# Encoder trunk on one core: x is turned before it is normalised, its loads are cut in halves, and the start of each layer is put in another order

## The chip, the cores and the metric

The kernel runs on one core of one Trainium2 chip. A core has TensorE (PE: matmuls and transposes, with PEld for its weight loads), VectorE (DVE), ScalarE (ACT), GpSimd (POOL) and SyncE (SP, which here only issues transfers). The metric is device time in microseconds (us), the median of several executions. One further execution was profiled; its span and rows are what the prediction works with.

## The reference

Input x is 256 tokens by 1024 features, f32. There are two layers; then a last RMS norm.

```python
for l in range(DEPTH):
    h = rms_norm(x, norm1_g[l])            # x * rsqrt(mean(x*x) + eps) * gain
    (aq, ..., k_rope) = jnp.split(h @ w_in[l], cuts, axis=-1)      # 1024 x 2144
    # four attentions o_a .. o_d from these, each 256 wide
    y = jnp.einsum('bsnc,ncd->bsnd', br, w_branch[l])
    g = jax.nn.sigmoid(h @ w_gate[l] + b_gate[l])                  # 1024 x 4096
    x = x + jnp.sum(g * y, axis=2) @ w_o[l]
    h2 = rms_norm(x, norm2_g[l])
    x = x + jnp.square(jax.nn.relu(h2 @ w_ff1[l])) @ w_ff2[l]
return rms_norm(x, final_g)
```

The root 1/sqrt(mean + eps) is one number for each token, so it can be multiplied in before a product with a weight matrix or behind it; the gain is one number for each feature.

## The kernel before

**Products.** All weights are f32 and are streamed once for each layer. Each is taken as a high part (`w_hi`, rounded to the matmul's f32r format) and the rest (`w_lo`), and so is each activation (`act_hi`, `act_lo`). A product is three matmuls: high by high, high by low, low by high (`split_product`, L1249 to L1251).

**Weight chunks.** A layer's weights come in chunks of about 1.05 MB, each as two halves. SP loads a half into `raw` (two chunks of room) as soon as DVE has split what stood there; ACT writes `w_hi` (`split_hi`, L603), and DVE writes `w_lo = raw - w_hi` (`split_lo`, L853). The first eight chunks are `w_in`, 268 columns each (`"in"`); a half of such a chunk holds four of the eight row blocks `kc`. Then come the gate and branch chunks, `w_o`, and the MLP.

**Start of a layer.** x lies as `xs` (128 tokens by 1024, twice: t = 0 and 1). ACT takes the sum of squares (`square_sum`, L613), POOL makes the root `rstd` (`norm`, L514 and L515), DVE and ACT scale x into `h` (L860 and L619), PE turns `h` by 128 x 128 transposes against an identity that is loaded first (`turn`, L1260) into four PSUM banks, ACT makes `act_hi` with the gain (`turned_hi`, L627 or L635), DVE makes `act_lo` (`turned_lo`, L871 or L880). Then PE forms chunk 0 by tokens 0 and 1 (`project`), chunk 1, and so on. The gains lie in `vec_all`: rows that were loaded, turned by PE (L1605) and copied (L1112). In the first layer `act_hi` and `act_lo` are made for both token blocks at once, 256 columns each. `keep_warm` issues matmuls whose result nobody reads. The sums of chunk j are taken out of PSUM by ACT for t = 0 (`in_evac`, L640) and by DVE for t = 1 (L1141).

**End of a layer.** The MLP's last two chunks are summed in eight parts of six matmuls with 512 columns (`mlp_out_last`). DVE adds each finished quarter to `xs` (`residual`, L892). In the first layer's end PE turns `h` of token block 0 in the middle of the last part, and block 1 inside the next layer's chunk 1 (`project_next_layer`).

**Order.** Each engine has its own program, written out by hand in this file, and works strictly in that order; a counter (semaphore) is waited for where one needs another's result. There is no scheduler. The gate stage adds the bias in `gate_add` (L1062); POOL loads the first two bias rows (`gate_bias`, L520) behind the root.

## Time and profile before

| | us |
|---|---|
| median of 3 runs | 827.41 (827.32 to 827.42) |
| profiled execution, device time | 827.35 |
| its span, first to last instruction | 825.5 |
| PE busy in the span | 813.9 |
| DVE, ACT, POOL busy | 549.8, 415.6, 56.6 |
| read from memory | 143.49 MB, 175 GB/s over the span |

The device time is 1.85 us above the span. Times in the rows count from the span's start. In a timeline row the first number is the start, the second how long it took (several of one kind merged, with their count at x), then engine, line, operation, output<-inputs, shape; in brackets how long the engine had been idle and whom it waited for.

### The profile page before, as it was taken

What the parts mean: (1) busy time and instruction counts of PE and PEld (TensorE: products, weight loads), DVE (VectorE), ACT (ScalarE), POOL (GpSimd) and SP (SyncE); (2) the same over time, 40 slices, a digit from 0 to 9 for tenths busy, and PEclk for the clock granted to TensorE, in tenths of its full rate; (3) what the DMA queues carried; (4) which work ended last, traced back from release to release, by engine and by line L of the source; (5) the groups of instructions that cost most, each with busy time, mean ns of one, the idle gap of its engine ahead of it and who ended that gap; (6) DMA issues with size and microseconds to landing.
All of it is one profiled execution on the core that took longest, in us unless ns stands there. A gap on an engine that the chain in (4) does not pass through costs nothing.

```text
span 825.5 us, 12984 instructions
## 1 busy us (share of the span) xinstructions
PE 813.9 (99%) x4835; PEld 701.8 (85%) x4835; DVE 549.8 (67%) x803; ACT 415.6 (50%) x698; POOL 56.6 (7%) x97
## 2 busy tenths in 40 slices
PE   7999999999999999999999999999999999999996
PEld 7997777877899999999899877678878999999995
DVE  6667768867676665555767577688774776555663
ACT  6455765664454444333563576658544544333442
POOL 2430000000010000000023200000000100000000
PEclk9999999999999999999999999999999999999999
DMA  8976653554357555565556747346344575566531
GB/s 275 230 232 201 182 179 108 153 170 157 103 173 234 172 173 175 193 203 203 173 149 194 250 163 216 105 139 172 106 168 129 187 243 171 188 203 202 180 126 52
DMA packets 85659, 145.14 MB, mean 176 GB/s; under 512 B 5036, under 2 KB 54448, under 8 KB 85616
## 3 DMA queue, kind: packets, MB, share of 16 engines
q1 hardware_dynamic: 82912, 137.12, 51.5%
q0 software_dynamic: 2496, 7.36, 3.3%
q8 instruction: 27, 0.44, 0.2%
q14 instruction: 16, 0.13, 0.1%
q10 hardware_dynamic: 208, 0.08, 0.0%
HBM read 143.49 MB, written 1.05 MB: 175 GB/s over the span
## 4 chain that ended last, share of the span: by engine, by line
PE 96%; DVE 1%; ACT 1%; POOL 1%; DMA 0%; issue 0%; POOLq 0%; ACTq 0%
PE bank_w L1249 20%; PE bank_w L1251 20%; PE bank_w L1250 20%; PE bank_acc L1249 8%; PE bank_acc L1250 8%; PE bank_acc L1251 8%; PE bank_acc L1345 2%; PE bank_o L1375 2%; PE bank_acc L1358 2%; DVE w_lo L853 1%; DMA cst<-in_table 0%; PE bank_acc L1260 0%; PE bank_x L1306 0%; PE bank_x L1327 0%; PE bank_x L1322 0%; POOL rstd L515 0%
## 5 line engine op out<-in xcount | busy, mean ns | idle before, releaser
L853 DVE TENSOR_TENSOR w_lo<-raw,w_hi 128x1024 fp32r<-128x1024 f32 (+1 forms) x256 | 301.9, 1228 | 61.8 <-ACT w_hi L603 61.4
L603 ACT ACTIVATE w_hi<-raw 128x1024 fp32r<-128x1024 f32 (+1 forms) x256 | 256.4, 1057 | 35.1 <-DMA raw<-in_w_gate 11.0
L1249 PE MATMUL bank_w<-w_hi,act_hi 128*128 128x268 f32 (+1 forms) x512 | 178.1, 348 | 0.1
L1251 PE MATMUL bank_w<-w_hi,act_lo 128*128 128x268 f32 (+1 forms) x512 | 173.9, 340 | 0.0
L1250 PE MATMUL bank_w<-w_lo,act_hi 128*128 128x268 f32 (+1 forms) x512 | 173.6, 339 | 0.0
L1251 PE MATMUL bank_w<-act_hi,w_lo 128*128 128x256 f32 x496 | 141.3, 285 | 0.0
L1250 PE MATMUL bank_w<-act_lo,w_hi 128*128 128x256 f32 x496 | 140.8, 284 | 0.0
L1249 PE MATMUL bank_w<-act_hi,w_hi 128*128 128x256 f32 x496 | 139.8, 282 | 0.0
L743 ACT ACTIVATE part_hi<-big 128x512 fp32r<-128x512 f32 x32 | 20.2, 633 | 189.2 <-DVE big L1095 186.5
L1249 PEld LDWEIGHTS bank_w<-w_hi,act_hi 128*128 128x128 f32 x512 | 96.2, 188 | 15.8 <-issue 6.2
L1251 PEld LDWEIGHTS bank_w<-w_hi,act_lo 128*128 128x128 f32 x512 | 96.2, 188 | 11.1
L1250 PEld LDWEIGHTS bank_w<-w_lo,act_hi 128*128 128x128 f32 x512 | 96.3, 188 | 10.2 <-issue 0.5
L1249 PE MATMUL bank_acc<-w_hi,part_hi 128*128 128x512 f32 x256 | 100.3, 392 | 0.0
L1250 PE MATMUL bank_acc<-w_lo,part_hi 128*128 128x512 f32 x256 | 100.3, 392 | 0.0
L1251 PE MATMUL bank_acc<-w_hi,part_lo 128*128 128x512 f32 x256 | 99.8, 390 | 0.0
L1095 DVE SCALAR_TENSOR_TENSOR big<-bank_w,root_row 128x512 f32<-128x512 f32 x30 | 20.7, 691 | 113.3 <-PE bank_w L1251 113.3
L1249 PEld LDWEIGHTS bank_w<-act_hi,w_hi 128*128 128x128 f32 x496 | 94.2, 190 | 1.2
L1250 PEld LDWEIGHTS bank_w<-act_lo,w_hi 128*128 128x128 f32 x496 | 93.5, 188 | 1.3
L1251 PEld LDWEIGHTS bank_w<-act_hi,w_lo 128*128 128x128 f32 x496 | 93.8, 189 | 0.0
L1251 PEld LDWEIGHTS bank_acc<-w_hi,part_lo 128*128 128x128 f32 x256 | 48.1, 188 | 10.6
L1249 PEld LDWEIGHTS bank_acc<-w_hi,part_hi 128*128 128x128 f32 x256 | 48.1, 188 | 9.5
L1250 PEld LDWEIGHTS bank_acc<-w_lo,part_hi 128*128 128x128 f32 x256 | 48.0, 188 | 8.9
(193 smaller groups left out, 890.5 us busy)
## 6 DMA issues: line engine op xcount, KB each, us to landing
raw<-in_w_ff SPq DMA_DIRECT2D x128, 512.0 KB, 4.9
raw<-in_w_gate SPq DMA_DIRECT2D x64, 512.0 KB, 4.7
raw<-in_w_in SPq DMA_DIRECT2D x32, 536.0 KB, 5.4
raw<-in_w_o SPq DMA_DIRECT2D x16, 512.0 KB, 4.5
gate_row<-in_b_gate POOLq DMA_DIRECT2D x16, 256.0 KB, 4.4
raw<-in_w_branch SPq DMA_DIRECT2D x16, 256.0 KB, 4.4
raw<-in_w_branch SPq DMA_DIRECT2D x8, 512.0 KB, 4.5
xs<-in_x SPq DMA_DIRECT2D x2, 512.0 KB, 4.2
```

Source lines behind the costliest of these rows:

```text
L603: nc.scalar.activation(half_view(w_hi, c, h), raw_half(c, h), ACT.Copy).then_inc(w_hi_ready, 1)
L743: nc.scalar.activation(part_hi[:, b, :, :].rearrange("p k s -> p (k s)"), relu[b], ACT.Square).then_inc(u_hi_ready, 1)
L853: nc.vector.tensor_tensor(half_view(w_lo, c, hf), raw_half(c, hf), f32(half_view(w_hi, c, hf)), ALU.subtract).then_inc(w_lo_ready, 1)
L1095: ins = nc.vector.scalar_tensor_tensor(out=relu[b].rearrange("p (d s) -> p d s", d=2), in0=bank_w[:, b, :].rearrange("p (d s) -> p d s", d ...
L1249: nc.tensor.matmul(dst, s_hi, m_hi, start=first, stop=False)
L1250: nc.tensor.matmul(dst, s_hi, m_lo, start=False, stop=False)
L1251: ins = nc.tensor.matmul(dst, s_lo, m_hi, start=False, stop=last)
L1345: ins = nc.tensor.matmul(bank_acc[:, half, keys], q[:, t * P:(t + 1) * P], k, start=True, stop=True)
L1358: ins = nc.tensor.transpose(bank_acc[:, 2 + b, at:at + P], prob[:, b, t, kt * P:(kt + 1) * P], ident)
L1375: ins = nc.tensor.matmul(bank_o[half * HD:(half + 1) * HD, blk * SEQ:(blk + 1) * SEQ], v, probT[:, half, kt, :], start=(kt == 0), stop=(kt ...
```

## The change

1. **x is turned raw.** `xs` itself is turned; `h`, its scaling on DVE and ACT (L860, L619) and the wait of PE for the root are gone at the start of both layers. The root is multiplied in later: where ACT and DVE take the sums of `w_in` out of PSUM, and in `gate_add`.
2. **Loads of the first layer.** x comes in four pieces of 128 x 512: both left halves, then the first half of chunk 0, then SP waits for the first piece, then both right halves, then the second half of chunk 0. The gain rows of the first norm are waited for alone; the others are turned later, behind chunk 1.
3. **First layer's order.** The five matmuls of `keep_warm` at the start are gone (two stay ahead of chunk 0). PE turns the left halves, takes the left half of chunk 0 by token block 0 in the order four high by high, four by `w_lo`, four by `act_lo`, turns the right halves, takes the left half for block 1, and so on. ACT and DVE make six `act_hi` / `act_lo` ahead of the second half of chunk 0, two behind it. Two of the four squares stand behind that.
4. **Second layer's order.** PE turns the quarters of x behind the residuals, between the parts of the MLP's last sum and between the first products; DVE's two splits of chunk 1 stand between the residuals, and its `act_lo` between them too.
5. POOL loads the first two gate bias rows behind the last small weight of the stage (`w_ukv`).

```diff
-PIECE_OF_FIRST = [(0, 0, D), (1, 0, D)]
+PIECES_OF_FIRST = [(0, 0, 512), (1, 0, 512), (0, 512, D), (1, 512, D)]
+FIRST_TURNED = [3, 4, 7, 8]
 SP:
+            load_x(0)
+            load_half(0, 0, 0)
+            sp.wait_ge(x_landed[0][0], 16)
+            load_x(1)
+            load_half(0, 1, 0)
 POOL:
                 norm(2 * l, l)
-                pool.wait_ge(gate_read, l * GATE_N)
-                for g in range(2):
-                    gate_bias(l, g)
 ...
                 pool.dma_start(w_ukv[:, :], d_w_ukv[bass.ds(l, 1)].rearrange("o k n -> (o k) n")).then_inc(lat_landed, 16)
+                pool.wait_ge(gate_read, l * GATE_N)
+                for g in range(2):
+                    gate_bias(l, g)
 ACT, in_evac:
+                if j == 0:
+                    act.wait_ge(rstd_ready, 2 * l * T + 1)
                 nc.scalar.activation(qkv[:, 0, j * IN_C:(j + 1) * IN_C], bank_w[:, in_bank(j, 0, l), 0:IN_C],
-                                     ACT.Copy).then_inc(in_act, 1)
+                                     ACT.Copy, scale=rstd[:, 0:1]).then_inc(in_act, 1)
 ACT, first layer:
             split_hi_half(0, 0, 0)
             act.wait_ge(vec_ready, 1)
-            turned_hi_both(0, G1, 0, range(0, KD // 2))
+            turned_hi_first(range(0, 6))
             split_hi_half(0, 1, 0)
-            turned_hi_both(0, G1, 0, range(KD // 2, KD))
-            split_hi(1, 0)
+            turned_hi_first(range(6, KD))
+            square_sum(0, 2)
+            split_hi_half(1, 0, 0)
+            square_sum(0, 3)
             in_evac(0, 0)
+            split_hi_half(1, 1, 0)
             split_hi(2, 0)
 ACT, second layer:
+                    turned_hi(2 * l, G1, l, 0, range(0, KD // 2))
                     square_sum(2 * l, 0)
+                    turned_hi(2 * l, G1, l, 0, range(KD // 2, KD))
                     square_sum(2 * l, 1)
-                    scale_right(2 * l, 0)
-                    turned_hi(2 * l, G1, l, 0, range(KD))
+                    in_evac(0, l)
 ...
 DVE, gate_add:
-                nc.vector.tensor_tensor(gate_slot(g // 2, 2 * t + g % 2), bank_w[:, t, :], gate_row[:, g % 2, :],
-                                        ALU.add).then_inc(gate_read, 1)
+                nc.vector.scalar_tensor_tensor(out=gate_slot(g // 2, 2 * t + g % 2), in0=bank_w[:, t, :],
+                                               scalar=rstd[:, t:t + 1], in1=gate_row[:, g % 2, :], op0=ALU.mult,
+                                               op1=ALU.add).then_inc(gate_read, 1)
 DVE, first layer:
-            for t in range(T):
-                scaled(0, t, 0).then_inc(h_ready, 1)
-                scaled(0, t, 1).then_inc(h_right_ready, 1)
+            gains(1, 0, DEPTH * KD)
             dve.wait_ge(vec_ready, 1)
             split_lo_half(0, 0, 0)
-            turned_lo_both(0, G1, 0, range(0, KD // 2))
+            turned_lo_first(range(0, 6))
             split_lo_half(0, 1, 0)
-            turned_lo_both(0, G1, 0, range(KD // 2, KD))
-            split_lo(1, 0)
+            turned_lo_first(range(6, KD))
+            split_lo_half(1, 0, 0)
+            split_lo_half(1, 1, 0)
 PE, new:
+            def turn_first(t, m):
+                pe.wait_ge(x_landed[t][m], 16)
+                turn(xs, t, 0, range(m * KD // 2, (m + 1) * KD // 2))
+            def project_high_parts_first(kcs):
+                pe.wait_ge(w_hi_ready, kcs[0] // (KD // 2) + 1)
+                for kc in kcs:
+                    pe.wait_ge(h_hi_ready, 2 * (kc + 1))
+                    nc.tensor.matmul(dst, act_hi[:, kc, tok], hi[:, kc, :], start=kc == 0, stop=False)
+                pe.wait_ge(w_lo_ready, kcs[0] // (KD // 2) + 1 + 2 * RAW)
+                for kc in kcs:
+                    nc.tensor.matmul(dst, act_hi[:, kc, tok], lo[:, kc, :], start=False, stop=False)
+                for kc in kcs:
+                    pe.wait_ge(h_lo_ready, 2 * (kc + 1))
+                    ins = nc.tensor.matmul(dst, act_lo[:, kc, tok], hi[:, kc, :], start=False, stop=kc == KD - 1)
             def project_first_layer():
-                for hf, kcs in enumerate((left, right)):
-                    pe.wait_ge(w_lo_ready, hf + 1 + 2 * RAW)
-                    project(0, 0, 0, kcs, [2 * (kc + 1) for kc in kcs])
-                    project(0, 1, 0, kcs)
+                project_high_parts_first(left)
+                turn_first(0, 1)
+                turn_first(1, 1)
+                project(0, 1, 0, left)
+                project_high_parts_first(right)
+                project(0, 1, 0, right)
 PE, mlp_out_last:
                 part(a, 2)
+                if l + 1 < DEPTH:
+                    turn_x(2 * l + 2, 0)
                 part(a, 3).then_inc(w_used, 1)
+                if l + 1 < DEPTH:
+                    turn_x(2 * l + 2, 1)
                 part(b, 2).then_inc(acc_done, 1)
-                if l + 1 < DEPTH:
-                    part(b, 3, (0,))
-                    turn_h(l + 1, 0)
-                    part(b, 3, (1,)).then_inc(w_used, 1)
 PE, start:
-            keep_warm(5)
-            turn_h(0, 0)
 ...
+            turn_first(0, 0)
+            turn_first(1, 0)
+            pe.wait_ge(rows_landed, 16)
+            turn_rows(DEPTH * KD)
             keep_warm(2)
```

**DVE at the first layer's start, before.** `xs`, `big` (holds `h`) and `rstd` as above.

```order
L860 TENSOR_SCALAR big<-xs,rstd 128x512 [waits rstd_ready] x4
L1112 COPY vec_all<-bank_acc 128x38 [waits rows_turned]
L853 TENSOR_TENSOR w_lo<-raw,w_hi 128x1072 [waits w_hi_ready,vec_ready]
L880 SCALAR_TENSOR_TENSOR act_lo<-bank_o,vec_all,act_hi 128x256 [waits h_hi_ready] x2
L880 SCALAR_TENSOR_TENSOR act_lo<-bank_x,vec_all,act_hi 128x256 [waits h_hi_ready] x2
L853 TENSOR_TENSOR w_lo<-raw,w_hi 128x1072 [waits w_hi_ready]
L880 SCALAR_TENSOR_TENSOR act_lo<-bank_acc,vec_all,act_hi 128x256 [waits h_hi_ready] x4
L853 TENSOR_TENSOR w_lo<-raw,w_hi 128x1072 [waits w_hi_ready] x2
L1141 COPY qkv<-bank_w 128x268 [waits w_used]
```

The same place with the change (line numbers are those of the changed file).

```order
L1114 COPY vec_all<-bank_acc 128x16 [waits rows_turned]
L865 TENSOR_TENSOR w_lo<-raw,w_hi 128x1072 [waits w_hi_ready,vec_ready]
L882 SCALAR_TENSOR_TENSOR act_lo<-bank_o,vec_all,act_hi 128x256 [waits h_hi_ready] x2
L882 SCALAR_TENSOR_TENSOR act_lo<-bank_x,vec_all,act_hi 128x256 [waits h_hi_ready] x2
L882 SCALAR_TENSOR_TENSOR act_lo<-bank_acc,vec_all,act_hi 128x256 [waits h_hi_ready] x2
L865 TENSOR_TENSOR w_lo<-raw,w_hi 128x1072 [waits w_hi_ready]
L882 SCALAR_TENSOR_TENSOR act_lo<-bank_acc,vec_all,act_hi 128x256 [waits h_hi_ready] x2
L865 TENSOR_TENSOR w_lo<-raw,w_hi 128x1072 [waits w_hi_ready] x2
L1148 TENSOR_SCALAR qkv<-bank_w,rstd 128x268 [waits rstd_ready,w_used]
```

The four scalings ahead are gone, and the second half's split of chunk 0 now stands behind six `act_lo` instead of four.

**PE at the first layer's start, with the change.** Before, the first product (L1249) stood behind all sixteen transposes and waited for `h_lo_ready` and `w_lo_ready`.

```order
L1267 MATMUL bank_o<-cst,xs 128x128 [waits x_landed1_0]
L1267 MATMUL bank_o<-cst,xs 128x128
L1267 MATMUL bank_x<-cst,xs 128x128 x2
L1627 MATMUL bank_acc<-cst,vec_rows 128x16 [waits rows_landed]
L1248 MATMUL bank_w<-cst 128x128 x2
L1401 MATMUL bank_w<-w_hi,act_hi 128x268 [waits h_hi_ready,w_hi_ready]
L1401 MATMUL bank_w<-w_hi,act_hi 128x268 [waits h_hi_ready] x3
L1404 MATMUL bank_w<-w_lo,act_hi 128x268 [waits w_lo_ready]
L1404 MATMUL bank_w<-w_lo,act_hi 128x268 x3
L1407 MATMUL bank_w<-w_hi,act_lo 128x268 [waits h_lo_ready] x4
L1267 MATMUL bank_acc<-cst,xs 128x128 [waits x_landed0_1]
```

The transposes of the right halves, and with them `act_hi` 4 to 7, now stand behind the four products with `act_lo` of the left half.

**DVE between the layers, before.**

```order
L853 TENSOR_TENSOR w_lo<-raw,w_hi 128x1072 [waits w_hi_ready] x4
L892 TENSOR_TENSOR xs<-xs,bank_acc 128x512 [waits acc_done] x2
L860 TENSOR_SCALAR big<-xs,rstd 128x512 [waits rstd_ready]
L892 TENSOR_TENSOR xs<-xs,bank_acc 128x512 [waits acc_done]
L871 SCALAR_TENSOR_TENSOR act_lo<-bank_o,vec_all,act_hi 128x128 [waits h_hi_ready] x2
L871 SCALAR_TENSOR_TENSOR act_lo<-bank_x,vec_all,act_hi 128x128 [waits h_hi_ready] x2
L892 TENSOR_TENSOR xs<-xs,bank_acc 128x512 [waits w_used]
```

With the change.

```order
L865 TENSOR_TENSOR w_lo<-raw,w_hi 128x1072 [waits w_hi_ready] x2
L894 TENSOR_TENSOR xs<-xs,bank_acc 128x512 [waits acc_done]
L865 TENSOR_TENSOR w_lo<-raw,w_hi 128x1072 [waits w_hi_ready]
L894 TENSOR_TENSOR xs<-xs,bank_acc 128x512 [waits acc_done]
L865 TENSOR_TENSOR w_lo<-raw,w_hi 128x1072 [waits w_hi_ready]
L873 SCALAR_TENSOR_TENSOR act_lo<-bank_o,vec_all,act_hi 128x128 [waits h_hi_ready] x2
L873 SCALAR_TENSOR_TENSOR act_lo<-bank_x,vec_all,act_hi 128x128 [waits h_hi_ready] x2
L894 TENSOR_TENSOR xs<-xs,bank_acc 128x512 [waits acc_done]
```

The first residual no longer stands behind four splits but behind two, and nothing here waits for the root.

## Rows read from the trace of the kernel before

**Rows 1.** The page: busy time of PE, and the chain by engine.

```profile
PE 813.9 (99%) x4835; PEld 701.8 (85%) x4835; DVE 549.8 (67%) x803; ACT 415.6 (50%) x698; POOL 56.6 (7%) x97
...
PE 96%; DVE 1%; ACT 1%; POOL 1%; DMA 0%; issue 0%; POOLq 0%; ACTq 0%
```

**Rows 2.** All waits of PE in the span: us in total, times, longest.

```profile
PE bank_w L1241 <- DMA cst<-in_table: 4.7, 1, 4.7
PE bank_o L1260 <- DVE big L860: 0.4, 1, 0.4
```

**Rows 3.** Timeline of PE, the first 12 us.

```profile
4.71 2.50 PE L1241 MATMUL bank_w<-cst 128*128 128x128 f32 x10 [4.71 <-DMA cst<-in_table]
...
7.63 0.64 PE L1260 MATMUL bank_x<-cst,big 128*128 128x128 f32 x2
8.05 1.06 PE L1260 MATMUL bank_acc<-cst,big 128*128 128x128 f32 x4
9.04 0.33 PE L1605 MATMUL bank_acc<-cst,vec_rows 38*128 38x38 f32 x1
...
11.03 0.61 PE L1241 MATMUL bank_w<-cst 128*128 128x128 f32 x4
11.69 0.36 PE L1249 MATMUL bank_w<-w_hi,act_hi 128*128 128x268 f32 x1
```

**Rows 4.** Timeline of ACT, the first 12 us.

```profile
7.76 1.10 ACT L603 ACTIVATE w_hi<-raw 128x1072 fp32r<-128x1072 f32 x1 [0.78 <-DMA raw<-in_w_in]
10.11 0.84 ACT L635 ACTIVATE act_hi<-bank_o,vec_all 128x256 fp32r<-128x256 f32 x2 [1.25 <-PE bank_o L1260]
```

**Rows 5.** Timeline of DVE, the first 24 us.

```profile
9.41 0.20 DVE L1112 COPY vec_all<-bank_acc 128x38 f32<-128x38 f32 x1 [0.33 <-PE bank_acc L1605]
9.64 1.27 DVE L853 TENSOR_TENSOR w_lo<-raw,w_hi 128x1072 fp32r<-128x1072 f32 x1
11.06 0.87 DVE L880 SCALAR_TENSOR_TENSOR act_lo<-bank_o,vec_all,act_hi 128x256 fp32r<-128x256 f32 x2 [0.15 <-ACT act_hi L635]
...
17.92 0.44 DVE L1141 COPY qkv<-bank_w 128x268 f32<-128x268 f32 x1
...
23.85 0.44 DVE L1141 COPY qkv<-bank_w 128x268 f32<-128x268 f32 x1 [3.13 <-PE bank_w L1251]
```

**Rows 6.** A stretch: length, busy time by engine, granted clock, DMA share, GB/s.

```profile
6.50:7.00 0.50, 0.50 (x4) 0.42 (x2) 0.40 (x1) 0.48 (x2) 0.07 (x1) 1.00 1.13 374
```

**Rows 7.** Timeline of DVE between the layers.

```profile
405.68 4.83 DVE L853 TENSOR_TENSOR w_lo<-raw,w_hi 128x1072 fp32r<-128x1072 f32 x4 [0.23 <-ACT w_hi L603]
410.42 1.27 DVE L892 TENSOR_TENSOR xs<-xs,bank_acc 128x512 f32<-128x512 f32 x2
413.47 0.48 DVE L860 TENSOR_SCALAR big<-xs,rstd 128x512 f32<-128x512 f32 x1 [1.77 <-POOL rstd L515]
...
416.79 1.12 DVE L871 SCALAR_TENSOR_TENSOR act_lo<-bank_acc,vec_all,act_hi 128x128 fp32r<-128x128 f32 x4
```

**Rows 8.** Timeline of ACT and of POOL between the layers.

```profile
411.13 0.63 ACT L613 ACTIVATE qkv<-xs 128x512 f32<-128x512 f32 x1 [2.53 <-DVE xs L892]
...
412.89 0.55 POOL L515 TENSOR_TENSOR rstd<-mean,neg_half 128x1 f32<-128x1 f32 x1
```

**Rows 9.** Timeline of PE between the layers.

```profile
413.24 0.40 PE L1251 MATMUL bank_acc<-w_hi,part_lo 128*128 128x512 f32 x1
414.01 0.44 PE L1260 MATMUL bank_o<-cst,big 128*128 128x128 f32 x2 [0.38 <-DVE big L860]
...
417.20 0.37 PE L1249 MATMUL bank_w<-w_hi,act_hi 128*128 128x268 f32 x1
417.41 0.28 PE L1250 MATMUL bank_w<-w_lo,act_hi 128*128 128x268 f32 x1
```

**Rows 10.** A stretch as in rows 6, and ACT's next split behind it.

```profile
55.00:56.00 1.00, 1.00 (x11) 1.00 (x10) 1.00 (x2) 0.00 (x0) 0.00 (x0) 1.00 0.18 70
...
57.42 2.94 ACT L603 ACTIVATE w_hi<-raw 128x1024 fp32r<-128x1024 f32 x3
```

100 lines of the change are left out of this document (48 added, 52 removed).

## The prediction

> **What bounds the kernel now.** First the page: PE is busy for 813.9 of 825.5 us, and the chain that ended last is PE to 96% [rows 1]. So I ask where PE is not at work, or works slowly. The list of its waits has two entries: 4.7 us for the identity, and 0.4 us for DVE's scaling of x between the layers [rows 2]. The other 6 or so of the 11.6 idle us lie behind the last matmul, in a tail that the change doesn't touch. A busy PE can still be slow, so I read the timeline of the first 12 us: ten records of `keep_warm` take 2.50 us, four later ones 0.61 [rows 3]. Each row ends with a tail of one record, so the pace was 0.23 us at 4.7 and 0.11 at 11.0; transposes stand 0.21 apart at 7.6 to 8.1, (8.05 - 7.63)/2 [rows 3]. The granted clock is printed as 1.00 there [rows 6], but a factor of two between equal records says that the array ran at its lower level (1.2 GHz) until about 11.0 and at 2.4 GHz from then on. The first product stands at 11.69 [rows 3]. From there PE needs 23.85 - 17.92 = 5.93 us for a chunk of 48 products, 0.1235 each [rows 5], without a pause. What counts for the time is therefore when chunk 1 ends (DVE takes it out at 23.85) and what PE loses between the layers.
>
> **First layer's start, step by step.** Removed: two squares, the root and four scalings ahead of the transposes. What is late next?
>
> Weights. The first half of chunk 0 was there at 7.7 [rows 4]; at 374 GB/s [rows 6] the 0.52 MB of x that no longer go ahead of it are worth 1.4 us: 6.3. It could be 5.9 (other packets less in the way) or 7.0 (x in shorter rows, 1.4 us saved only by half).
>
> PE and the gains. Identity at 4.7 as now; eight transposes at 0.21: 6.4; the rows (0.26 by 9.04 to 9.30 in the order above): 6.7; copy [rows 5]: 7.1. ACT splits from 6.35 to 7.45 (1.10 [rows 4]), then makes `act_hi` 0 to 3, 0.37 apart. PE's first product is at 7.9 in place of 11.69. That looks like 3.8 us, but PE then works for whom? For DVE.
>
> DVE's queue. `w_lo` of the half from 7.5 (1.27, the next can start 1.18 after it), four `act_lo` at 0.40 each (0.87 for two [rows 5]): 8.7 to 10.4. PE follows with the last of four `act_lo` products at 10.8 (products at the lower clock 0.22, twice 0.11). Only then it turns the right halves: 8 x 0.106 at the higher clock, 11.9. ACT: `act_hi` 4 and 5, to 12.65; split of the second half, 12.6 to 13.7; `act_hi` 6 and 7, to 14.4. DVE has stood still from 10.4 to 12.75. It makes two `act_lo`, `w_lo` of the second half from 13.75 to 15.0, two `act_lo` to 15.8, then needs the halves of chunk 1, and these are late on ACT: square 14.3, split 15.0 to 16.05, square to 16.6 (0.63 each [rows 8]), `in_evac` (0.4) to 17.0, split to 18.0. DVE: 16.1 to 17.4 and 18.05 to 19.3. PE: left half for block 1 to 13.5, pause, right half of block 0 to 16.1, of block 1 to 17.6, chunk 1 left to 19.1, pause for `w_lo` until 19.4; then 12 + 24 products x 0.1235 = 4.45, the last issued at 23.85, its sums out at 24.1. That is **0.25 us later** than 23.85. The 3.8 us are eaten by the order of ACT and DVE: the second half of chunk 0 was split at about 12.5 and is now split at 13.7, and chunk 1 is cut in two by squares and `in_evac`. With the weights at 7.0 the same walk gives +0.65; at 5.9 it gives +0.1, since PE's low clock then holds it. If in addition the clock rose at 7.6, -0.4.
>
> The copies with a root in them cost what the plain ones cost (0.44 against 0.48 for a scaling of 512 columns [rows 5, 7]), and the engines have 3.1 us of slack ahead of each [rows 5]: 0. The root is ready at 16.0 and 17.6, ahead of both users: 0. The second turning of the rows is one more PE step between chunk 1 and 2: 0.33 alone at the lower clock [rows 3], so 0.1, between 0 and 0.2; the loads that it waits for are tens of us old by the pace of rows 3.
>
> **Gate stage.** `gate_add` gets a multiply: 0.69 for such an operation from PSUM, as now to within 0.02, and hidden by PE. The two bias rows (0.5 MB, 1.4 us of the queue) now come at about 49 us, beside the last small weight and the gate chunks. At 55 to 56 the queue runs at 70 GB/s, so it had caught up, and ACT splits the next chunk only at 57.42, without a wait [rows 10]: room of about 1.5 to 2 us, just enough. 0, at worst +0.4 twice.
>
> **Between the layers.** Now: four splits on DVE to 410.5, two residuals (0.62 apart) [rows 7], squares, root at 413.4 [rows 8], scaling at 413.47 [rows 7]. PE issued a part's product at 413.24 and could have gone on at 413.47; it turned from 414.01 [rows 9]: 0.54 lost. At 417.20 one product stands 0.21 ahead of the next in place of 0.12, and starts late too [rows 9]: about 0.2, `act_lo` behind a residual. With the change: two splits to 408.1; the first quarter is done at 407.2 on PE (12 parts products at 0.23 behind the 18 before); residual 408.1 to 408.75; PE turns it at 410.0. Split, residual 409.9 to 410.6; PE turns it at 411.8. Split to 411.7, four `act_lo` at 0.26 [rows 7] to 413.0, residual at 413.8, four `act_lo` to 415.5. PE reaches the next layer's first product at 414.95; `act_lo` 0 is there since 412, number 4 is wanted at 416.4 and there at 414.8. The quarters of block 1 are wanted at 417.9 and 419.8 and there at 414.5 and 416.1; their `act_lo` are wanted from 421.7, there from 419.5. ACT's takeout of chunk 1 stands behind its split of chunk 2, at 423.9 to 424.3, wanted at 424.7: 0.4 us of room. No pause is left. **Gain 0.54 + 0.2, say 0.75**, between 0.4 (one new pause) and 0.8. Nothing is gained from fewer transposes: there are as many.
>
> **Sum** against the profiled execution's own 827.35: +0.25 + 0.1 - 0.75 = -0.4, so 826.95; it stands 0.06 below the median shown: **827.0**.
>
> **Rivals.**
> 1. *The clock rises later.* It rose at 11.0 after 6.3 us in which PE had hardly paused, `keep_warm` first, transposes after [rows 3]. Now those five matmuls are gone, and between 7.9 and 9.2 the products come 0.37 apart. If the low stretch is counted from the first product, it ends at 7.9 + 6.3 = 14.2: the eight transposes and block 1's left products run at half speed, `act_hi` 4 comes 0.7 later, and so does all behind it: 827.7. The Trainium skill (TensorE: Matmul & The Clock Gate, Part 4) says that transposes don't count as PE being busy, and this would be its outcome; but in this trace the rise came at the end of a stretch in which PE had only turned [rows 3], which speaks against it. Chance 0.24.
> 2. *PE alone is the limit.* If ACT and DVE keep up, chunk 1 ends 3.8 - 0.85 (eight transposes now between products) earlier: 23.85 - 2.95, and with the rest 823.7; half of it gives 825.2. Against it stand the four pieces of DVE's queue above; for it only that weights at 5.9 and an early clock take 0.65 off. Chance of anything below 825.75: 0.12.
> 3. *A little earlier*: weights or clock early as priced above, 826.3. Chance 0.14.
> 4. *Slower.* The pauses keep the clock low into chunk 1. Each product at the lower level costs 0.1 more; the 24 of block 1 and block 0's right half, then twelve and more of chunk 1 in sequence: with a rise at 21 chunk 1 ends 3.3 later: 830.0. It decides from a rise at about 19 on (+1.7). Against it: DVE is then idle, PE dense, and a dense PE got its clock within 6.3 us. Chance 0.07.
> 5. *The gain between the layers fails*: 827.6, within rival 1's span; chance 0.05.
>
> **How the numbers follow.** Forecast, 826.5 to 827.5: 0.38. Rivals 1, 3 and 5 end within 0.2% of 827.41 (825.75 to 829.05), which is about what a measurement of this kernel can tell from no change. Same: 0.38 + 0.24 + 0.14 + 0.05 = 0.81. Faster 0.12, slower 0.07. The range takes in rival 1 with late weights (14.2 and 7.0: 828.4) and rival 3 with all of its bounds (825.9): 825.8 to 828.4, which leaves out rivals 2 and 4.
>
> **What would show it.** Right: first product near 7.9, a PE pause in chunk 0's middle and one near 19 for `w_lo`, DVE idle about 2.3 us behind its fourth `act_lo`, the takeout of chunk 1 at 24.1, no wait of PE between the layers. Wrong: a takeout of chunk 1 before 22.5 (rival 2), transposes of the right halves 0.21 apart (rival 1), PE waiting for `act_lo` or for chunk 9's split.

## The result: slower by a quarter of a per cent

The changed kernel takes 829.2 us (median of 16 executions, 828.59 to 829.82). In the same session the kernel before took 827.38 (16 executions). The ratio is 1.0024, with a 95% interval of 1.0017 to 1.0031. The prediction was 827.0, with a range up to 828.4, and "no change": the change is slower, and the time lies outside the range. The profiled execution of the changed kernel took 829.72 us, that of the kernel before 827.35, 2.4 apart. So about 0.5 of what separates the two traces belongs to these two executions and not to the kernels.

The page of the changed kernel, the lines that answer to [rows 1] (first the busy time, then the chain that ended last):

```profile
PE 814.8 (98%) x4826; PEld 701.3 (85%) x4826; DVE 554.0 (67%) x798; ACT 416.2 (50%) x700; POOL 55.1 (7%) x99
...
PE 91%; DVE 4%; ACT 2%; DMA 1%; issue 1%; POOL 1%; SPq 0%; POOLq 0%; ACTq 0%; DVEq 0%
```

PE is as busy as before, but 5% of the chain have gone from PE to engines that it waits for, and to the issue of instructions. All its waits (us in total, times, longest), which answer to [rows 2]:

```profile
PE bank_o L1267 <- DMA cst<-in_table: 4.1, 1, 4.1
PE bank_w L1401 <- ACT act_hi L641: 1.4, 1, 1.4
PE bank_w L1401 <- ACT w_hi L615: 0.3, 1, 0.3
PE bank_w L1256 <- DVE big L1064: 0.3, 1, 0.3
PE bank_w L1404 <- DVE w_lo L865: 0.2, 1, 0.2
PE bank_w L1256 <- DVE w_lo L865: 0.2, 1, 0.2
```

The wait between the layers is gone; but for the one for the identity (`cst`) the others are new. To see where the time went I set the same instruction of both traces side by side, DVE's takeouts of the chunks of `w_in` and its first `gate_add` of each layer (start in us):

| instruction on DVE | before | changed | lag |
|---|---|---|---|
| takeout of chunk 1, layer 1 | 23.85 | 25.98 | 2.13 |
| chunk 5 | 47.58 | 49.81 | 2.23 |
| chunk 7 | 60.10 | 62.78 | 2.68 |
| chunk 1, layer 2 | 428.76 | 430.69 | 1.93 |
| chunk 7, layer 2 | 465.00 | 466.93 | 1.93 |
| first `gate_add`, layer 2 | 477.15 | 479.35 | 2.20 |
| last `gate_add`, layer 2 | 607.34 | 609.65 | 2.31 |

The first two rows of this table don't part the start from the second turning of the gain rows. With the change DVE's takeout of chunk 1 stands behind its copy of those rows, which before has no counterpart. So I take PE's own rows at the end of chunk 1, changed and then before:

```profile
25.38 0.28 PE L1258 MATMUL bank_w<-w_hi,act_lo 128*128 128x268 f32 x1
25.59 0.25 PE L1627 MATMUL bank_acc<-cst,vec_rows 38*128 38x38 f32 x1
25.77 0.39 PE L1256 MATMUL bank_w<-w_hi,act_hi 128*128 128x268 f32 x1
26.00 0.29 PE L1257 MATMUL bank_w<-w_lo,act_hi 128*128 128x268 f32 x1
```

```profile
23.52 0.28 PE L1251 MATMUL bank_w<-w_hi,act_lo 128*128 128x268 f32 x1
23.65 0.28 PE L1249 MATMUL bank_w<-w_hi,act_hi 128*128 128x268 f32 x1
23.77 0.28 PE L1250 MATMUL bank_w<-w_lo,act_hi 128*128 128x268 f32 x1
```

and DVE's copy with the takeout behind it (changed):

```profile
25.88 0.18 DVE L1114 COPY vec_all<-bank_acc 128x22 f32<-128x22 f32 x1 [2.23 <-PE bank_acc L1627]
25.98 0.49 DVE L1148 TENSOR_SCALAR qkv<-bank_w,rstd 128x268 f32<-128x268 f32 x1
```

The last product of chunk 1 is 1.86 late, and two products on it is 2.23. So five numbers make up the loss: +1.86 at the start (forecast +0.25); +0.37 for the second turning of the rows (forecast 0.1, between 0 and 0.2), of which 0.27 already stand in the lag of chunk 1's takeout; +0.45 and +0.4 in the two gate stages (forecast 0, "at worst +0.4 twice"); and -0.75 between the layers (as forecast).

**The start.** PE's timeline of the changed kernel, which answers to [rows 3]:

```profile
8.86 1.60 PE L1401 MATMUL bank_w<-w_hi,act_hi 128*128 128x268 f32 x4 [1.37 <-ACT act_hi L641]
10.25 1.10 PE L1404 MATMUL bank_w<-w_lo,act_hi 128*128 128x268 f32 x4
11.15 1.10 PE L1407 MATMUL bank_w<-w_hi,act_lo 128*128 128x268 f32 x4
12.04 1.53 PE L1267 MATMUL bank_acc<-cst,xs 128*128 128x128 f32 x8
```

ACT's timeline, which answers to [rows 4]:

```profile
7.25 1.10 ACT L615 ACTIVATE w_hi<-raw 128x1072 fp32r<-128x1072 f32 x1 [1.55 <-DMA raw<-in_w_in]
...
13.45 0.84 ACT L641 ACTIVATE act_hi<-bank_acc,vec_all 128x256 fp32r<-128x256 f32 x2 [3.63 <-PE bank_acc L1267]
14.18 1.10 ACT L615 ACTIVATE w_hi<-raw 128x1072 fp32r<-128x1072 f32 x1
```

DVE's timeline, which answers to [rows 5]:

```profile
8.46 1.28 DVE L865 TENSOR_TENSOR w_lo<-raw,w_hi 128x1072 fp32r<-128x1072 f32 x1 [1.91 <-ACT w_hi L615]
...
10.44 0.87 DVE L882 SCALAR_TENSOR_TENSOR act_lo<-bank_x,vec_all,act_hi 128x256 fp32r<-128x256 f32 x2
14.39 0.88 DVE L882 SCALAR_TENSOR_TENSOR act_lo<-bank_acc,vec_all,act_hi 128x256 fp32r<-128x256 f32 x2 [3.09 <-ACT act_hi L641]
...
19.61 1.27 DVE L865 TENSOR_TENSOR w_lo<-raw,w_hi 128x1072 fp32r<-128x1072 f32 x1 [0.70 <-ACT w_hi L615]
```

Read them as a circle. DVE has made its fourth `act_lo` at 11.3. PE takes it, turns the right halves until 13.5, ACT makes `act_hi` 4 and 5 and only then splits the second half of chunk 0, at 14.18. ACT has stood idle for 3.63 us and DVE for 3.09. Two of PE's numbers say more. The first product stands at 8.86, since the weights were there at 7.25. And four products of 268 columns take 1.10 us with a tail of one record, 0.22 apart, where at the higher clock they stand 0.12 apart. Eight transposes take 1.53, in place of 1.91 where all are slow (e5 below) or 1.03 where all are fast (e16): the array went from its lower level (1.2 GHz) to 2.4 in the middle of them, at about 13.0. Before, it did so at 11.0.

**The gate stage.** DVE's timeline of the changed kernel from 50 us, then POOL's:

```profile
51.41 5.08 DVE L865 TENSOR_TENSOR w_lo<-raw,w_hi 128x1072 fp32r<-128x1072 f32 x1
```

```profile
51.15 0.55 POOL L532 DMA_DIRECT2D gate_row<-in_b_gate  x1
51.72 0.95 POOL L576 TENSOR_TENSOR bias<-tmp,cst 128x384 f32<-128x384 f32 x1
...
54.39 0.95 POOL L576 TENSOR_TENSOR bias<-tmp,cst 128x384 f32<-128x384 f32 x1
```

A split that takes 1.27 us took 5.08. It was running when POOL began its four bias adds, and it ended 1.15 us behind the last of them. The same place before (DVE, then POOL):

```profile
49.12 2.02 DVE L853 TENSOR_TENSOR w_lo<-raw,w_hi 128x1072 fp32r<-128x1072 f32 x1
```

```profile
48.45 1.55 POOL L564 TENSOR_TENSOR bias<-tmp,cst 128x384 f32<-128x384 f32 x1
49.96 1.95 POOL L564 TENSOR_TENSOR bias<-tmp,cst 128x384 f32<-128x384 f32 x1
```

There the first two adds waited (0.95 alone, 1.55 and 1.95 here), and the split took 2.02. In both traces the two engines take turns on such operands (0.31 us of the split, 3.6 of adds and 1.14 of the split add up to its 5.08); what differs is who goes first. The Trainium skill (SBUF — State Buffer, "SBUF: two separate sides") has DVE and GpSimd share one port pair as an exclusive lock, taken by a `tensor_tensor` with both inputs in SBUF as well. This agrees. It also says that whoever starts first keeps the pair for the whole instruction, and here the trace disagrees: the split had started 0.31 us ahead of the adds and lost.

**The second gate stage** looks different. No split there takes over 1.77 us in this trace, so the +0.4 is no held split. PE waits for a `gate_add`. DVE itself has been 2.2 us late from 476.16 on, where it waited for a split of ACT, and ACT for a load; PE's timeline, then ACT's (before, this split of ACT started at 472.86 behind a wait of 1.50 us):

```profile
488.70 0.50 PE L1256 MATMUL bank_w<-w_hi,act_hi 128*128 128x512 f32 x1 [0.27 <-DVE big L1064]
```

```profile
475.07 1.06 ACT L615 ACTIVATE w_hi<-raw 128x1024 fp32r<-128x1024 f32 x1 [1.74 <-DMA raw<-in_w_gate]
```

Before, PE's product stood at 486.37, so it is 2.33 late here, where the takeouts ahead of it were 1.93 late. Whether the load was late because of the bias rows, of POOL's adds or by chance, and what the root's 60 ns (e7) add, no run here tells apart.

**Between the layers.** PE's timeline of the changed kernel, which answers to [rows 9] (DVE's residual now starts at 410.72, with a split on either side):

```profile
412.47 0.39 PE L1258 MATMUL bank_acc<-w_hi,part_lo 128*128 128x512 f32 x1
412.70 0.38 PE L1267 MATMUL bank_o<-cst,xs 128*128 128x128 f32 x2
...
413.05 0.48 PE L1256 MATMUL bank_acc<-w_hi,part_hi 128*128 128x512 f32 x1
```

The transposes stand 0.23 behind the last product of a part, as the next product would, and PE waits for nobody here. Taken over this stretch alone, from DVE's last takeout of the MLP ahead of it (403.29 before, 405.97 changed) to its takeout of chunk 0 (426.27 and 428.22), the lag falls by 0.73; it does so in each of the 15 other traces with this order (e11 keeps the old one: 0.03).

### The profile page after: what moved, and what is told of

It is laid out like the page before. It is cut to its first block, busy times and chain, and to the rows that moved or that the text cites. A ratio compares the mean times of both kernels' runs of the same rounds, so it can differ in the third digit from the quotient of the medians.

```text
span 827.9 us, 12976 instructions
## 1 busy us (share of the span) xinstructions
PE 814.8 (98%) x4826; PEld 701.3 (85%) x4826; DVE 554.0 (67%) x798; ACT 416.2 (50%) x700; POOL 55.1 (7%) x99
## 4 chain that ended last, share of the span: by engine, by line
PE 91%; DVE 4%; ACT 2%; DMA 1%; issue 1%; POOL 1%; SPq 0%; POOLq 0%; ACTq 0%; DVEq 0%
PE bank_w L1256 19%; PE bank_w L1258 18%; PE bank_w L1257 18%; PE bank_acc L1256 9%; PE bank_acc L1257 9%; PE bank_acc L1258 9%; DVE w_lo L865 2%; PE bank_acc L1350 2%; PE bank_o L1380 2%; PE bank_acc L1363 2%; ACT w_hi L615 1%; DMA raw<-in_w_in 1%; DMA raw<-in_w_gate 1%; PE bank_x L1332 0%; PE bank_x L1327 0%
## 5 line engine op out<-in xcount | busy, mean ns | idle before, releaser
L865 DVE TENSOR_TENSOR w_lo<-raw,w_hi 128x1024 fp32r<-128x1024 f32 (+1 forms) x256 | 306.1, 1244 | 64.4 <-ACT w_hi L615 64.1
L615 ACT ACTIVATE w_hi<-raw 128x1024 fp32r<-128x1024 f32 (+1 forms) x256 | 256.9, 1057 | 36.9 <-DMA raw<-in_w_gate 12.5
L1256 PE MATMUL bank_w<-w_hi,act_hi 128*128 128x512 f32 (+1 forms) x504 | 176.0, 349 | 0.5 <-DVE big L1064 0.3
L1258 PE MATMUL bank_w<-w_hi,act_lo 128*128 128x512 f32 (+1 forms) x504 | 171.6, 340 | 0.0
L1257 PE MATMUL bank_w<-w_lo,act_hi 128*128 128x512 f32 (+1 forms) x504 | 171.3, 340 | 0.0
L1258 PEld LDWEIGHTS bank_acc<-w_hi,part_lo 128*128 128x128 f32 x256 | 48.1, 188 | 10.6
```

The source lines that it names most:

```text
L615: nc.scalar.activation(half_view(w_hi, c, h), raw_half(c, h), ACT.Copy).then_inc(w_hi_ready, 1)
L865: nc.vector.tensor_tensor(half_view(w_lo, c, hf), raw_half(c, hf), f32(half_view(w_hi, c, hf)), ALU.subtract).then_inc(w_lo_ready, 1)
L1256: nc.tensor.matmul(dst, s_hi, m_hi, start=first, stop=False)
L1257: nc.tensor.matmul(dst, s_hi, m_lo, start=False, stop=False)
L1258: ins = nc.tensor.matmul(dst, s_lo, m_hi, start=False, stop=last)
```

## The experiments

All are the changed kernel with an edit, but e11. For each: DVE's takeout of chunk 1 and of chunk 7 (layer 1) in its trace, where PE's clock rose (read from the distance of equal records, to about 0.2 us), its profiled time, and the median and ratio.

| kernel | chunk 1 | chunk 7 | clock rose | profiled | median | ratio (95%) |
|---|---|---|---|---|---|---|
| before | 23.85 | 60.10 | 11.0 | 827.35 | 827.38 | 1 |
| changed | 25.98 | 62.78 | 13.0 | 829.72 | 829.2 | 1.0024 (1.0017-1.0031) |
| e1 | 25.62 | 61.97 | 12.5 | 828.44 | 829.27 | 1.0027 (1.0017-1.0038) |
| e2 | 26.02 | 62.82 | 15.1 | 830.37 | 829.47 | 1.0029 (1.0019-1.0039) |
| e3 | 23.73 | 60.08 | 10.7 | 826.31 | 827.11 | 0.9999 (0.9990-1.0008) |
| e7 | 25.79 | 62.78 | 12.9 | 829.03 | 828.92 | 1.0021 (1.0012-1.0030) |
| e4 | 25.07 | 62.03 | 8.0 | 828.78 | 828.47 | 1.0016 (1.0007-1.0025) |
| e5 | 25.79 | 62.73 | 13.7 | 829.39 | 829.39 | 1.0028 (1.0019-1.0038) |
| e6 | 23.54 | 59.89 | 11.6 | 826.41 | 827.22 | 1.0002 (0.9993-1.0011) |
| e8 | 25.88 | 62.23 | 13.8 | 829.73 | 829.93 | 1.0036 (1.0023-1.0050) |
| e12 | 25.27 | 61.63 | 11.8 | 828.57 | 828.82 | 1.0018 (1.0009-1.0027) |
| e9 | 25.66 | 62.01 | 15.4 | 828.96 | 826.96 | 0.9993 (0.9984-1.0002) |
| e10 | 24.19 | 60.54 | 9.2 | 827.54 | 827.42 | 1.0003 (0.9994-1.0012) |
| e11 | 23.84 | 60.07 | 10.8 | 827.10 | 827.18 | 0.9999 (0.9990-1.0008) |
| e13 | 22.45 | 58.80 | 9.5 | 825.41 | 825.51 | 0.9982 (0.9973-0.9991) |
| e14 | 24.41 | 60.75 | 13.4 | 827.11 | 826.78 | 0.9992 (0.9983-1.0001) |
| e15 | 23.64 | 60.72 | 12.0 | 827.91 | 826.06 | 0.9986 (0.9977-0.9995) |
| e16 | 24.68 | 61.37 | 10.6 | 828.24 | 828.24 | 1.0011 (1.0002-1.0020) |

Two things have to be kept in mind. An interval is about 0.8 us to either side, so two ratios 0.0005 apart are not told apart. And one profiled execution can lie 2 us off the median of its kernel (e9, e15), so a lag in one trace need not be its kernel's. All rows but before and e11 have the copy of the rows ahead of chunk 1's takeout, which is 0.27 of their distance from before.

### First: the gate stage, the old start, the root

**e1.** POOL's bias rows go back behind the root.

```diff
                 norm(2 * l, l)
+                pool.wait_ge(gate_read, l * GATE_N)
+                for g in range(2):
+                    gate_bias(l, g)
```

> The changed kernel with one part undone: POOL issues the two gate bias rows behind the root, as before, and not behind w_ukv. In the changed kernel one w_lo split on DVE took 5.08 us at 51.4 while POOL, just behind the two issues, made its four bias adds; before, the longest split there took 2.02. Theory A (DVE is held up beside POOL's adds, and the two issues shifted the adds onto the next split): the longest split between 47 and 60 us falls back to about 2.0, the lag against the kernel before stops growing at the first-layer takeouts j=6, 7 (0.4 less) and at the second layer's gate stage (0.3 less): 828.5, ratio 1.0014. Theory B (the root in gate_add and in the copies is what costs): 829.2 as the changed kernel, ratio 1.0024. Theory C (the 0.5 MB of bias rows beside the gate chunks holds the queue): also 828.5, but the split on DVE may stay long.

In the trace the split took 2.02, and the lag stayed (1.77 at chunk 1, 1.87 at chunk 7, 1.09 behind the boundary and 1.08 in layer 2's gate stage). By the trace theory A holds; by the median, 829.27, nothing was gained. The profiled execution was the fastest of eight. Left open at this point.

**e2.** The bias rows behind the four adds (the `for g in range(2)` stands behind `bias_ready`).

> The two gate bias rows are issued behind POOL's four bias adds, so the adds start 1.1 us earlier than in the changed kernel, at the same place against DVE's splits as before, while the 0.5 MB comes even later beside the gate chunks. Theory A (DVE held up beside POOL's adds): the longest split is back at about 2.0 us, 828.5, ratio 1.0014. Theory C (the queue): the gate chunks are late as in the changed kernel or worse, 829.2 or above, and the load at 57 us still is waited for. Theory B (the root's multiply): 829.2.

The adds began 0.31 us into a split in the first layer and 0.32 in the second, and a split was held in both. DVE's timeline:

```profile
50.27 5.08 DVE L864 TENSOR_TENSOR w_lo<-raw,w_hi 128x1072 fp32r<-128x1072 f32 x1
...
456.34 5.10 DVE L864 TENSOR_TENSOR w_lo<-raw,w_hi 128x1072 fp32r<-128x1072 f32 x1
```

My expectation for theory A was wrong in its number, since I took it that being earlier helps. But a held split appears here without the bias rows ahead of it, so the adds hold it and not these transfers. The median, 829.47, is also what theory C (the queue) had: whether the 0.5 MB cost something of their own isn't decided.

**e3.** The old start: whole x and all halves loaded at once, `keep_warm(5)`, all transposes first, ACT and DVE in the old order. The bias rows are back behind the root as well, as in e1. Of the edit, PE's part and the loads:

```diff
-            load_half(0, 0, 0)
-            sp.wait_ge(x_landed[0][0], 16)
-            load_x(1)
-            load_half(0, 1, 0)
+            keep_warm(5)
             turn_first(0, 0)
             turn_first(1, 0)
 ...
+            turn_first(0, 1)
+            turn_first(1, 1)
             keep_warm(2)
```

> The first layer's start is put back: x in two whole loads with all weight halves right behind, keep_warm(5), all sixteen transposes ahead of the first product, ACT and DVE in the order of before (four, the second half's split, four, chunk 1, then the takeout), bias rows behind the root. x is still turned raw, the root still comes at the evictions, and the second layer's order stays as changed. My theory (the new start costs 2.1 us, the boundary gives 0.75 back): the first takeout of DVE is at 16.8 and chunk 1's at 22.7, some 1.1 before the kernel before, since act_hi waits no longer for turned rows and scaled x (8.9 in place of 10.1), and the time is 827.4 - 1.1 - 0.75 + 0.2 for the slower copies = 825.7, ratio 0.998. Rival (what costs is the raw turning and the root in the evictions, not the start's order): no better than 827.4, ratio 1.000.

827.11: 2.0 us better than the changed kernel, so the loss is in the start (its order, its loads and the clock together, and the bias rows with them), and neither in the raw turning nor in the root at the takeouts. But it is no better than before, where I expected 825.7. Its first product stood at 11.29 against 11.69 [rows 3], behind the sixteen transposes, which PE issues as late as ever, and the last product of chunk 1 at 23.12 against 23.52. These 0.40 us then went into the second turning of the rows: two products later the lead is 0.02. That step costs 0.37 to 0.38 us here as in the changed kernel.

**e7.** The root is left out of the takeouts and of `gate_add` (plain copies and a plain add), so its numbers lack the root.

> The changed kernel with the root left out of the eight takeouts of w_in and out of gate_add in both layers (plain copies and a plain add, as before), so the numbers lack the root; nothing else differs. Theory B (the multiply costs, copies 0.06 and gate_add 0.06 us longer each, and the lag grew by 0.05 to 0.07 at single gate_adds of the second layer): 0.3 to 0.4 us less than the changed kernel, 828.8, ratio 1.0018. Theory A (only POOL against DVE): 829.2 within 0.1, ratio 1.0024, and one split near 51 us still takes about 5 us.

1.0021 against 1.0024: 0.25 us by ratio, less than can be told apart. The groups of DVE in the changed kernel (mean ns behind the comma):

```profile
L1064 DVE SCALAR_TENSOR_TENSOR big<-bank_w,rstd,gate_row 128x512 f32<-128x512 f32 x32 | 23.9, 746 | 4.9 <-PE bank_w L1258 4.9
L1148 DVE TENSOR_SCALAR qkv<-bank_w,rstd 128x268 f32<-128x268 f32 x16 | 7.9, 495 | 21.0 <-PE bank_w L1258 21.0
```

In e7 they are 686 and 435 ns. The multiply costs 60 ns in each, 2.9 us of DVE in all. Ahead of the takeouts DVE waits for PE for 21.0 us and has room for it; ahead of the `gate_add` it waits for 4.9 in all, so not every one has. In e7's trace PE doesn't wait for a `gate_add`, and the lag doesn't grow in the second gate stage (1.79 at chunk 7, 1.72 at the last `gate_add`); but in e1's, with the multiply, it doesn't either (1.09 and 1.06). A split still took 5.33 us at 51.16, as theory A had it.

### Second: what in the start costs

**e4.** `keep_warm(5)` back ahead of the transposes.

> The changed kernel with the five matmuls of keep_warm put back ahead of the first transposes. In the traces so far PE ran at its lower clock until 12.6 to 15.0 us in the four kernels with the new start and until 11.0 and 10.7 in the two with the old one. Theory (part of the 2.1 us of the start is the clock that rises later, because PE has pauses): PE is busy from 4.0 to 7.5 without them, the rise comes at about 10.3, the transposes of the right halves take 0.85 us in place of 1.5, the takeout of chunk 1 comes 0.9 earlier (+1.2 against the kernel before), 828.3, ratio 1.0012. Rival (the order of PE, ACT and DVE alone): five matmuls more ahead cost nothing and give nothing, 829.2, ratio 1.0024.

The takeout moved by the 0.9 expected (25.98 to 25.07). The median gained 0.7 by ratio; e16 asks the same in a better place.

**e5.** The right halves are issued behind the first half of chunk 0.

```diff
-            sp.wait_ge(x_landed[0][0], 16)
+            sp.wait_ge(landed[0][0], 16)
             load_x(1)
```

> SP issues the right halves of x only when the first half of chunk 0 has landed, and not when the first piece of x has. Theory (the half was there at 7.25 in place of 6.3 because the right halves, issued at 3.9, were served beside it): it lands by 6.2, the first product moves from 8.86 to 7.9, the takeout of chunk 1 comes 0.8 earlier (+1.3 against the kernel before) if the right halves, issued at 6.2, are there by 9.5: 828.4, ratio 1.0013. Rival (PE's clock is what holds the first products: they start earlier but end where they did): takeout of chunk 1 within 0.2 of the changed kernel, 829.2, ratio 1.0024.

The rival was right: 829.39. ACT could split the half at 6.76 in place of 7.25, and the first product stood at 8.36, but the array stayed slow until 13.7, and the transposes took 1.91 in place of 1.53 us. In this trace the clock took most of what the weights gave, and the median shows no gain.

**e6.** The right halves are turned ahead of the first product.

```diff
                 project_high_parts_first(left)
-                turn_first(0, 1)
-                turn_first(1, 1)
                 project(0, 1, 0, left)
 ...
             turn_rows(DEPTH * KD)
+            turn_first(0, 1)
+            turn_first(1, 1)
             keep_warm(2)
```

> PE turns the right halves of x ahead of the first products, all else as in the changed kernel. Theory (the loss is the order: act_hi 4 and 5, and behind them the split of the second half, wait until PE has been through the twelve left products): act_hi 4 and 5 follow act_hi 3 directly, the second half's split starts at about 12.2 in place of 14.18, chunk 1 is split 2 us earlier, its takeout comes 1.8 earlier (+0.3 against the kernel before): 827.4, ratio 1.0002. Rival (clock and weights): the first product moves back by 0.4 us, nothing else moves by more than 0.5: 829.2 to 829.6, ratio 1.0027.

1.0002, as the theory had it, and its marks are in the rows. ACT and then DVE:

```profile
11.15 1.10 ACT L615 ACTIVATE w_hi<-raw 128x1072 fp32r<-128x1072 f32 x1 [0.62 <-DMA raw<-in_w_in]
```

```profile
17.17 1.27 DVE L865 TENSOR_TENSOR w_lo<-raw,w_hi 128x1072 fp32r<-128x1072 f32 x1 [1.28 <-ACT w_hi L615]
```

The second half is split at 11.15 and not at 14.18, though the first product comes 1.5 later (10.33). PE waits for nobody from its first product on. One edit of order gives 1.8 us by ratio. In this trace the clock also rose at 11.6 and not at 13.0, so not all of the distance between the two traces is the order; e9 has the same start with a late rise.

**e8.** POOL's adds wait for the split of chunk 8.

```diff
                 pool.wait_ge(bias_landed, l * 32 + 32)
+                pool.wait_ge(w_lo_ready, lo_count(l, 8))
```

> POOL's four bias adds wait until DVE has split chunk 8, so they fall into DVE's idle stretch of 3 us before its next takeout (they are wanted 35 us later); the bias rows stay where the change put them. In five traces the adds began in the middle of two splits at 47 to 56 us, and in three of them one split was held for 5.1 to 5.3 us, until the four adds were over; in the others it took 1.3 or 2.0. Theory (this is the loss in the gate stage, and in most executions of the changed kernel it happens): no split over 1.4 us, the lag stays constant from the takeout of chunk 2 to the layer's end, 828.5, ratio 1.0014. Rival (the loss in most executions is elsewhere, as the median of the run with the bias rows put back, 829.27, suggests): 829.2, ratio 1.0024.

Worse, 829.93. ACT got chunk 8's second half late, so the adds began at 61.5 and ran into the next splits. POOL and DVE then took turns at 1.9 us each, and PE waited 1.0 us for `w_lo`. In the second layer the gap was met and no split was over 1.3. Only five executions were taken. The place was badly chosen; the theory is not touched by it.

### Third: adds where DVE is idle, and a start without holes

**e12.** Bias rows as in e1, and the adds wait for the split of chunk 7 (`lo_count(l, 7)`).

> The changed kernel, start and boundary as changed, but the bias rows back behind the root, and POOL's four bias adds wait until DVE has split chunk 7; DVE is idle for some 3 us then. In the nine traces so far that start the adds while a split runs, the adds got through in 3.63 us and held the split for 5.1 to 5.3 us in five, and DVE kept its split (1.3 to 2.1 us) in the others. Theory (which of the two happens differs from one execution to the next, so the medians of the earlier runs hold a mixture of it, and only a place where nothing overlaps takes it away): no split over 1.4 us there in either layer, and the median 0.7 below the changed kernel's: 828.5, ratio 1.0014. Rival (the profiled executions with a held split are not the usual ones, the median's loss is elsewhere): 829.2, ratio 1.0024.

No split over 1.3 in either layer; the lag is 1.53 at chunk 5 and 1.53 at chunk 7. POOL's timeline, the adds right behind the split they wait for:

```profile
52.16 3.63 POOL L576 TENSOR_TENSOR bias<-tmp,cst 128x384 f32<-128x384 f32 x4 [0.99 <-DVE w_lo L865]
```

The median lies between the two theories (1.0018). Not decided.

**e9.** e12 and e6 together.

> The same two edits on POOL, and PE turns the right halves of x ahead of the first products. Right halves early alone gave 827.22 in the median and 826.41 in its profiled execution, in which no split was held. Theory (the median lacks 0.8 because in most executions a split is held): 826.4, ratio 0.9992. Rival (not from there): 827.2, ratio 1.0002.

0.9993 against 0.9992 forecast. Its profiled execution is the slowest of eleven, and shows one way in which executions of one kernel come to differ. PE's timeline:

```profile
9.51 1.12 PE L1267 MATMUL bank_acc<-cst,xs 128*128 128x128 f32 x4 [0.68 <-DMA xs<-in_x]
...
15.07 0.43 PE L1258 MATMUL bank_w<-w_hi,act_lo 128*128 128x268 f32 x1
15.30 0.35 PE L1256 MATMUL bank_w<-w_hi,act_hi 128*128 128x268 f32 x1
```

The same products of the same start stand 0.22 apart up to 15.3. The second piece of x was late, PE had a second hole, and the takeout of chunk 1 came at 25.66, in e6 at 23.54. Against e6 the adds' new place gives 0.75 us by ratio and 0.26 by median, again within the intervals.

**e10.** e9, and three `keep_warm` in PE's wait for the right halves, the two behind the transposes gone; ACT's order split, square, split, takeout, square.

> The previous kernel, and at the start: three matmuls of keep_warm in PE's wait of 1.4 us for the right halves of x, the two behind the transposes gone, and ACT splits both halves of chunk 1 ahead of what stood between them (the order is now split, square, split, takeout, square). Theory (with the order mended, what is left of the start is PE itself, its low clock, and the late split of chunk 1's second half): the first product at 9.6 in place of 10.33, chunk 1's takeout 0.8 earlier than with the right halves early alone (-1.1 against the kernel before): 825.6, ratio 0.9982. Rival (DVE's act_lo, to 11.3 and 14.4, holds PE): it starts earlier but the takeout moves by 0.2 only: 826.3, ratio 0.9990.

The product started at 9.65 as expected, and nine of eleven executions lay within 0.4 us. But the median was 827.42: the change of ACT's order made a new wait. POOL's timeline:

```profile
14.45 0.88 POOL L526 TENSOR_TENSOR mean<-mean 128x1 f32<-128x1 f32 x1 [9.45 <-ACT qkv L625]
15.40 1.64 POOL L527 TENSOR_TENSOR rstd<-mean,neg_half 128x1 f32<-128x1 f32 x1
```

and ACT's (PE waited 1.4 us for this takeout):

```profile
17.14 0.48 ACT L648 ACTIVATE qkv<-bank_w,rstd 128x268 f32<-128x268 f32 x1 [1.83 <-POOL rstd L527]
```

The root's two operations on a single column took 0.88 and 1.64 us beside two splits of DVE, against 0.20 and 0.57 in e13.

**e11.** The kernel before with the adds behind chunk 7's split.

> The kernel before, with one edit: POOL's four bias adds wait until DVE has split chunk 7. In its profiled execution the adds began 0.52 us into a split in the first layer, and DVE kept it (2.02 us at most). Theory (a held split is rare here, so the kernel before hardly suffers, and the change made it common by putting the adds 0.3 us into a split): 827.2 as the kernel before, ratio 1.0000 within 0.0005. Rival (before suffers in many executions as well): 826.7, ratio 0.9994 or below.

0.9999: the kernel before doesn't suffer from the adds.

### Fourth: order, clock and POOL apart

**e13.** e10 with ACT in the order square, split, split, takeout, square. ACT's part against the changed kernel:

```diff
             square_sum(0, 2)
             split_hi_half(1, 0, 0)
-            square_sum(0, 3)
-            in_evac(0, 0)
             split_hi_half(1, 1, 0)
+            in_evac(0, 0)
+            square_sum(0, 3)
```

> Right halves of x turned early, three matmuls of keep_warm in PE's wait, bias rows and adds as in e9, and ACT in the order square, split, split, takeout, square. In e10 the square stood behind the first split, POOL's root then ran beside two splits of DVE (0.88 and 1.64 us in place of 0.20 and 0.57), ACT's takeout waited for it until 17.1 and PE 1.4 us for ACT. Theory: the root is there at 14.3, PE has no wait in chunks 0 and 1 behind its first product, chunk 1 is taken out 1.4 earlier than in e10 (-1.06 against the kernel before): 826.0, ratio 0.9985. Rival (the second root, for DVE's takeout, now is what comes late, or w_lo of chunk 1's second half): a new wait of about 1 us, 827.0, ratio 0.9996.

825.51, ratio 0.9982 (0.9973 to 0.9991): faster than both kernels, by ratio 1.5 us faster than before and 3.5 faster than the changed one. PE's timeline:

```profile
8.95 0.94 PE L1267 MATMUL bank_acc<-cst,xs 128*128 128x128 f32 x4 [0.15 <-DMA xs<-in_x]
9.64 0.75 PE L1401 MATMUL bank_w<-w_hi,act_hi 128*128 128x268 f32 x4
```

The root's operations, at 13.58 and 13.85, are back at 0.20 and 0.57, and apart from the identity only 0.2 us of wait is left to PE in the whole execution.

**e14.** e9 with the fill alone (ACT's order as changed).

> As e9 (right halves early, adds in DVE's idle time) and only PE's wait filled with three matmuls of keep_warm, the two behind it gone; ACT's order as changed, with squares and takeout between the two splits of chunk 1. Theory (the clock rises by 10 and not anywhere from 11 to 15, and the spread between executions shrinks): first product at 9.65, then 0.8 us of wait for the late w_lo of chunk 1's second half, takeout of chunk 1 at -0.3; the median 826.5 with most executions within 0.5 us, ratio 0.9991. Rival (the fill costs what it gives): 827.0 with the spread of e9, 1.5 us.

The median fits (0.9992), the spread doesn't (825.2 to 828.05). In its trace the second right piece of x landed at 9.7, 1.0 us of wait stayed behind the fill, and the clock rose at 13.4. The fill helps only where it covers the whole hole.

**e15.** e13 with POOL as changed.

> The start of e13, but the bias rows and POOL's adds where the change has them. Theory (a split of DVE held by the adds in one layer or both, 0.3 to 0.6 us each time): 0.6 above e13, 826.6, ratio 0.9992, and in its profile a split of over 5 us near 50. Rival (POOL's part costs nothing in most executions): the same as e13 within 0.2.

826.06 against 825.51 for e13 in the same session: 0.35 by ratio, 0.55 by median, in the forecast direction, though the intervals overlap. Its trace has a split of 5.37 us at 49.08 and a lag that grows by 0.7 from chunk 5 to chunk 7.

**e16.** The changed kernel with `keep_warm(5)` for `keep_warm(2)` ahead of the first product.

> The changed kernel with keep_warm(5) in place of keep_warm(2) ahead of the first product, so PE has no pause from 4.0 to 8.9; all else as changed. Theory (clock and order share the loss): the clock rises by 10, the transposes of the right halves take 0.9 in place of 1.5 us, the takeout of chunk 1 moves from +2.1 to +1.2, the spread between executions shrinks: 828.3, ratio 1.0012. Rival (order alone): 829.2, ratio 1.0024.

828.24 and 1.0011, all eleven executions within 0.6 us (the changed kernel's 16 within 1.2). PE's timeline:

```profile
6.27 2.50 PE L1248 MATMUL bank_w<-cst 128*128 128x128 f32 x10
8.52 1.60 PE L1401 MATMUL bank_w<-w_hi,act_hi 128*128 128x268 f32 x4
9.91 0.98 PE L1404 MATMUL bank_w<-w_lo,act_hi 128*128 128x268 f32 x4
11.25 1.03 PE L1267 MATMUL bank_acc<-cst,xs 128*128 128x128 f32 x8
```

PE has no hole from 4.1 to 14, the clock rose at about 10.6, and the transposes take 1.03 and not 1.53. Matmuls that compute nothing gave 1.1 us by ratio. The order is still the changed one, and the last product of chunk 1 stands at 24.08, 0.56 behind before and not 1.86. (0.34 of that difference is there from the first product on, since the weights came earlier in this execution.)

## Why the prediction was wrong

**The start, +0.25: the mis-sized term, measured +1.86.** (The forecast's last product of chunk 1, 23.85, stands 0.33 behind the 23.52 of before; the 0.25 was read from the takeout.) The steps were those that the walk described: DVE idle behind its fourth `act_lo`, the second half's split late, a pause for `w_lo` near 19. Two of its inputs were off. The weights came at 7.25 and not at 6.3, outside the bounds (5.9 to 7.0); even without the right halves beside them they came at 6.76 (e5), so the 1.4 us for 0.52 MB less ahead of them was too much. And the clock rose at 13.0 and not at 11.0. Both add up along one chain: last left product 12.0 (forecast 10.8), transposes to 13.5 (11.9), second half's split at 14.18 (12.6), chunk 1's second `w_lo` at 19.61 (18.05). e16 keeps the order and fills PE's hole: chunk 1 then ends within 0.25 us of the forecast. So the walk through the queues was about right for the clock that it assumed, and that clock was the step that failed most. The order had its part too: e6 and e3, which undo it, are 1.8 and 2.0 us faster than the changed kernel. But in their traces the clock rose earlier as well, and e3 moves the bias rows, so how much is order and how much is clock stays open; the two are not independent, since where PE has a hole follows from the order.

**The clock is rival 1, and it came true in kind.** The walk kept "11.0 as before" although the change removed the very five matmuls that filled PE's first microseconds and opened a hole of 1.4 us. e16 prices it: 1.1 us by ratio, where rival 1 had 0.7. What I had against rival 1, that PE only turned when the clock rose before, was no argument for 11.0: in the traces in which PE stood still for 0.7 us or more between 6 and 10 us (changed, e1, e2, e5 to e9, e12, e14) the rise came at 11.6 to 15.4, and in those with less (before, e3, e4, e10, e11, e13, e15, e16) at 8.0 to 12.0. The two ranges overlap, so this goes with the hole and isn't shown to be ruled by it alone. The Trainium skill (TensorE: Matmul & The Clock Gate, Part 4) doesn't let transposes count as work for the clock. These runs don't decide that: in e4 the rise came at the end of a row of eight transposes, but ten records of matmuls stood ahead of them.

**The second turning of the rows, 0.1 (0 to 0.2): mis-sized too, measured 0.37.** The walk counted the transpose alone. Around it PE's records stand 0.21, 0.18 and 0.23 apart in place of 0.12 and 0.12.

**Copies and `gate_add`, 0.** Each costs 60 ns more, as was not foreseen. By e7 it is 0.25 us or nothing; that all of it is hidden by PE isn't shown, since PE waits once for a `gate_add` (0.27 at 488.70).

**Gate stage, 0 and at worst +0.4 twice: the worst came.** I had looked for the 0.5 MB on the queue. In the first layer POOL counted: the adds moved onto a running split. With POOL as changed, six of the seven traces (changed, e4, e5, e7, e15, e16, but not e6) have a split of 5.0 to 5.4 us in the first layer; with the bias rows at the old place (before, e1, e3) none has one over 2.1. What it costs in the median is less sure: 0.35 to 0.55 (e15 against e13), 0.5 (e12 against changed), 0.25 to 0.75 (e9 against e6), each within the intervals, and nothing in e1. Why e1's median shows no gain stays open, and so does the cause of the +0.4 in the second layer.

**Between the layers, -0.75: right**, 0.73 in each of the 16 traces that have this order.

**The sum.** 1.86 + 0.37 + 0.45 - 0.73 + 0.4 is 2.35, and the two profiled executions are 2.4 apart. The range had late weights and a late clock together in it (7.0 and 14.2: 828.4), but the late clock at a price of 0.7, where e16 gives 1.1 for a rise at 13.0. It put the rows at 0.2 at most and held the gate stage at nil, and all of these lie on the same side.

## What to carry to other kernels

When work is taken from the front of a kernel, ask what it was covering: the matmuls removed here kept PE without a hole, and without them the clock came 2 us later in the trace. Give an engine nothing to do that waits for a result of the engine which waits for it, while work with no such tie stands behind in its queue (right halves turned behind the left products: 1.8 us, the clock's share in it included). Read what a step costs from the engine that bounds the stage, and not from a takeout behind it: a single small transpose between two chunks cost PE 0.37 us. And an operation on POOL that reads the same memory as DVE belongs where DVE is idle: here a small one beside two splits took three to four times its time, and four in a row could hold a split for as long as they lasted.

## What the runs showed of the hardware that was not expected

- A DVE `tensor_tensor` on 1072 columns, both inputs in SBUF, takes 1.27 us alone, 2.0 to 2.1 when it alternates with POOL's adds, and 4.96 to 5.37 when it is running as they begin and loses (eight times in seven traces). It lost with a head start of 0.19 to 0.59 us and kept its place with 0.52 (before, e3) and 0.85 or more; what decides between them isn't known.
- POOL's power on one column: 0.57 us alone (e13), 1.64 beside two splits (e10).
- With one and the same start the clock rose at 11.6 in one execution (e6) and at 15.4 in another (e9); the takeout of chunk 1 differed by 2.1 us. In e9 PE had a second hole of 0.68 us, for a piece of x that landed late. The granted clock is printed as 1.00 in the slow stretch too ([rows 6] has it for before), so only the distance of equal records shows it.
- A load issued 2.2 us behind another seems to be served beside it: with the right halves of x held back (e5) ACT could split the first half of chunk 0 at 6.76, and in the fourteen traces in which they were issued at 3.8 to 4.5 at 6.91 to 7.29. That is one trace against fourteen.
- A transpose of 38 x 38 put between two rows of products cost PE 0.37 to 0.38 us (changed, e3), though PE stood idle at neither side of it by the trace.
